# An fp32 transformer step on one Trainium2 core: token tiles finished one by one, side work and copies reordered, router products turned, slot rows on another queue

## The reference

```python
def first_block(x, ...):
    h = layer_norm(x, ln_in_g, ln_in_b)
    for l in range(2):
        m = hybrid_mixer(h, w_in[l], cmp_pos[l], cmp_w1[l], ..., w_o[l])
        h = layer_norm(ALPHA * h + m, ln1_g[l], ln1_b[l])
        if l % 2 == 0:
            f = swiglu(h, ffn_wg[0], ffn_wu[0], ffn_wd[0])              # 1024 -> 2816 -> 1024
        else:
            f = moe_swiglu(h, moe_router[0], moe_wg[0], moe_wu[0], moe_wd[0])
        h = layer_norm(ALPHA * h + f, ln2_g[l], ln2_b[l])
    return h

def hybrid_mixer(h, w_in, ...):
    q, kc, vc, ks, vs, kw, vw, gates, u, bg, cg = jnp.split(h @ w_in, offsets, axis=-1)
    # q goes to three attentions: over compressed keys (an MLP over blocks of kc, vc),
    # over selected blocks (ks, vs), over a window (kw, vw); u, bg, cg to a short convolution
    return jnp.concatenate([o_attn, o_conv], axis=-1) @ w_o

def moe_swiglu(h, w_router, wg, wu, wd):
    top_v, top_i = lax.top_k(h @ w_router, 2)                           # 8 logits a token
    gate = jnp.sum(jax.nn.one_hot(top_i, 8) * softmax(top_v)[..., None], axis=-2)
    return sum(gate[..., e:e + 1] * swiglu(h, wg[e], wu[e], wd[e]) for e in range(8))

def second_block(x, c, ...):
    shift, scale, gate = jnp.split(silu(c) @ w_mod + b_mod, 3, axis=-1)
    h = rms_norm(x, g_norm) * (1.0 + scale) + shift
    # projections of h; convolution and RG-LRU; rotary dilated attention in three groups
    x = x + gate * (merged @ w_o)
    return rms_norm(x, g_final)
```

## Time and profile before

| | |
|---|---|
| runs | 2350.46, 2355.13, 2360.42 us (median 2355.13) |
| the profiled execution | 2353.95 us; its span 2352.1 us |
| granted TensorE clock, mean | 0.988 |
| busy: PE | 2294.8 us, 98% |
| busy: PEld (weight loads) | 1824.2 us, 78% |
| busy: DVE (VectorE) | 1459.4 us, 62% |
| busy: ACT (ScalarE) | 1185.2 us, 50% |
| busy: POOL (GpSimd) | 553.8 us, 24% |
| DMA | 435.51 MB, mean 185 GB/s |

### The profile page before, as it was taken

One profiled execution on the slowest core, in us unless ns is written; L12 is line 12 of the kernel. 1 busy time (PEld: TensorE's weight loads), 2 busy tenths in 40 slices (PEclk: granted clock), 3 DMA queues, 4 the chain that ended last, 5 costly groups with the idle time before them and its releaser, 6 DMA issues.

```text
span 2352.1 us, 30586 instructions
## 1 busy us (share of the span) xinstructions
PE 2294.8 (98%) x11059; PEld 1824.2 (78%) x11059; DVE 1459.4 (62%) x2159; ACT 1185.2 (50%) x1625; POOL 553.8 (24%) x230
## 2 busy tenths in 40 slices
PE   7999999999999999999999999999989999999998
PEld 5766777788888766688888888888866788788787
DVE  5277674621163576688889888898887572245333
ACT  4344342222233444377778777777764652334323
POOL 4212334544422221210000000000023344433342
PEclk9999999999999999999999999999998999999999
DMA  8211237823324211379999999999982233322232
GB/s 231 54 46 46 72 108 244 277 78 97 106 85 126 61 45 43 138 281 375 369 388 381 384 366 379 387 386 379 356 315 63 72 99 100 95 65 72 71 91 72
DMA packets 321096, 435.51 MB, mean 185 GB/s; under 512 B 15024, under 2 KB 259168, under 8 KB 320992
## 3 DMA queue, kind: packets, MB, share of 16 engines
q1 hardware_dynamic: 301356, 402.58, 49.1%
q10 hardware_dynamic: 17332, 23.17, 3.2%
q0 software_dynamic: 2304, 8.39, 0.9%
HBM read 409.97 MB, written 22.02 MB: 184 GB/s over the span
## 4 chain that ended last, share of the span: by engine, by line
PE 86%; DVE 6%; DMA 4%; ACT 2%; issue 1%; ACTq 0%; DVEq 0%; SPq 0%
PE bank L841 21%; PE bank L1284 18%; PE bank L845 10%; PE bank L1295 8%; PE bank L1463 6%; PE bank L1158 5%; DMA mod_raw<-in_w_mod_dram 2%; PE bank L1194 2%; PE bank L1133 2%; PE bank L1175 2%; DMA raw_m<-in_moe_wu_dram 1%; PE bank L1303 1%; DVE mod_sum L2255 1%; PE bank L1042 1%; PE bank L882 1%
## 5 line engine op out<-in xcount | busy, mean ns | idle before, releaser
L778 POOL TENSOR_TENSOR rest<-raw,head 128x1024 fp32r<-128x1024 f32 (+1 forms) x210 | 529.8, 2528 | 1025.3 <-ACT head L1593 997.2
L2543 DVE TENSOR_TENSOR rest_m<-raw_m,head_m 128x1408 fp32r<-128x1408 f32 (+1 forms) x405 | 576.4, 1458 | 86.0 <-ACT head_m L1663 81.3
L1663 ACT ACTIVATE head_m<-raw_m 128x1408 fp32r<-128x1408 f32 (+1 forms) x405 | 495.6, 1251 | 111.1 <-DMA raw_m<-in_moe_wu_dram 38.6
L1593 ACT ACTIVATE head<-raw 128x1024 fp32r<-128x1024 f32 (+1 forms) x210 | 225.7, 1077 | 247.8 <-PE bank L845 178.0
L841 PE MATMUL bank<-HH,head 128*128 128x512 f32 x760 | 307.0, 404 | 8.3 <-ACT head L1593 4.2
L841 PE MATMUL bank<-HL,head 128*128 128x512 f32 x760 | 301.2, 396 | 0.0
L1284 PE MATMUL bank<-head_m,XH 128*128 128x512 f32 x720 | 277.0, 385 | 0.7 <-DVE rest_m L2543 0.7
L1284 PE MATMUL bank<-head_m,XL 128*128 128x512 f32 x720 | 270.4, 375 | 0.0
L1284 PE MATMUL bank<-rest_m,XH 128*128 128x512 f32 x720 | 270.3, 375 | 0.0
L845 PE MATMUL bank<-HH,rest 128*128 128x512 f32 x760 | 192.7, 395 | 0.0
L841 PEld LDWEIGHTS bank<-HH,head 128*128 128x128 f32 x760 | 143.0, 188 | 49.0 <-issue 10.8
(11 more groups left out here) (459 smaller groups left out, 3845.6 us busy)
## 6 DMA issues: line engine op xcount, KB each, us to landing
raw_m<-in_moe_wg_dram SPq DMA_DIRECT2D x120, 704.0 KB, 8.0
raw_m<-in_moe_wu_dram SPq DMA_DIRECT2D x120, 704.0 KB, 7.0
raw_m<-in_moe_wd_dram SPq DMA_DIRECT2D x165, 512.0 KB, 5.2
raw<-in_w_in_dram SPq DMA_DIRECT2D x110, 512.0 KB, 4.0
raw<-in_w_o_dram SPq DMA_DIRECT2D x24, 512.0 KB, 4.0
mod_raw<-in_w_mod_dram ACTq DMA_DIRECT2D x12, 1024.0 KB, 6.6
raw<-in_ffn_wg_dram SPq DMA_DIRECT2D x22, 512.0 KB, 3.9
raw<-in_ffn_wu_dram SPq DMA_DIRECT2D x22, 512.0 KB, 3.9
```

The source lines that it names most:

```text
L778: pool.tensor_tensor(rest[slot][:, 0:kt, :], raw[slot][:, 0:kt, :], head[slot][:, 0:kt, :], ALU.subtract).then_inc(weights_split, 1)
L1593: act.activation(head[slot][:, 0:kt, :], raw[slot][:, 0:kt, :], ACT.Copy).then_inc(head_done, 1)
L1663: act.activation(head_m[at_ % HEADS_M][:, 0:w], raw_m[at_ % RAWS][:, 0:w], ACT.Copy) \
L2543: dve.tensor_tensor(rest_m[at_ % RAWS][:, 0:w], raw_m[at_ % RAWS][:, 0:w], head_m[at_ % HEADS_M][:, 0:w], ALU.subtract).then_inc(gran_spli ...
```

## The change

1. **Token tiles one by one.** For each of the four tiles statistics and offset (VectorE), root and normalization (ScalarE) are written together; VectorE now normalizes the whole of the last tile.
2. **Vector loads.** The seven on ScalarE's queue go to SP's, behind `vectors_in`'s own, and SP waits for token tile 1 ahead of the first weight tile.
3. **Query bank.** Query tile 0 is taken ahead of the copies from K in both layers.
4. **Side work.** `side_loads(j - 1)` stands ahead of the copy of `UH[j]`, and `mod_chunk(j - 1)` is summed after pair j.
5. **Norms.** Two subtractions are written ahead of the wait for the deviation.
6. **Router.** The tokens are the stationary side, the 8 weight columns the moving one: 32 products of 8 columns, whose result already has tokens on the partitions; `lgT`, its copy and the four transposes are gone, and the semaphore counts with them.
7. **Slot rows.** Those of slot 1 are issued by ScalarE, ahead of its last silu of slot 0; SP goes on with its granules.

```diff
+RAW_BEHIND = 1
-STAT_AT = [1, 2, 4, 7]
-OFF_AT = [3, 5, 6, 8]
+STAT_AT = [1, 3, 5, 7]
+OFF_AT = [2, 4, 6, 8]
...
                 for g in range(first):
                     granule(g, owner[0])
-                sp.wait_ge(x_scattered, 16 * 2 * ST)
-                slot_rows(1)
                 stored = 0
...
-                for name, rows in VECTORS[VECTORS_SP:]:
+                for name, rows in VECTORS[EARLY:]:
+                    if name == "b2dup":
+                        continue
...
+                if l == 0:
+                    sp.wait_ge(sem_x[RAW_BEHIND], 16)
                 for k, c in enumerate(order):
...
                 for k in range(KT):
                     pe.wait_ge(h_ready, 2 * KT + k + 1)
-                    last = pe.matmul(bank[6][0:EXPERTS, :], rw[:, k, :], H[:, k, :], start=(k == 0), stop=(k == KT - 1))
+                    for t in range(ST):
+                        last = pe.matmul(bank[6][:, t * EXPERTS:(t + 1) * EXPERTS], H[:, k, t * P:(t + 1) * P], rw[:, k, :],
+                                         start=(k == 0 and t == 0), stop=(k == KT - 1 and t == ST - 1))
...
-                for q in range(2):
+                for q in range(2 * ST):
                     tokens(q)
+
                 pe.wait_ge(lg_ready, 2)
-                for t in range(ST):
-                    last = pe.transpose(bank[7][:, t * EXPERTS:(t + 1) * EXPERTS], lgT[:, t * P:(t + 1) * P],
-                                        cst[0:EXPERTS, 0:EXPERTS])
-                last.then_inc(lg_done, 1)
-                for q in range(2, 2 * ST):
-                    tokens(q)
-
-                pe.wait_ge(lg_ready, 3)
                 ranks = bank[7][:, 64:64 + TE]
...
-            for name, rows in VECTORS[EARLY:VECTORS_SP]:
-                if name != "b2dup":
-                    st, row = WHERE[name] // P, WHERE[name] % P
-                    act.dma_start(stage[row:row + rows, st, :], vector_sources(a, name)).then_inc(sem_stage, 16)
...
+                act.wait_ge(x_scattered, 16 * 2 * ST)
+                act.dma_start(xs[1][:, :], x_rows[P:2 * P, :]).then_inc(xs_landed[1], 16)
                 silu(0, KT - 1)
-                act.wait_ge(x_scattered, 16 * 2 * ST)
...
-            x_root(0)
-            x_root(1)
-            x_normed(0, 0, D)
-            x_root(2)
-            x_normed(1, 0, D)
-            x_normed(2, 0, S)
-            x_root(3)
-            x_normed(2, S, D)
-            x_normed(3, S, D)
+            for t in range(ST - 1):
+                x_root(t)
+                x_normed(t, 0, D)
+            x_root(ST - 1)
...
                         ahead(e, 2 * j + 1)
+                        if after and j >= 1:
+                            after(j - 1)
                         act.wait_ge(bank_free[(n + 1) % RING], e * (N_PART // RING) + (n + 1) // RING + 1)
                         act.activation(UH[:, j, :], gu[:, j % 2, :], ACT.Copy).then_inc(uh_ready, 1)
-                        if after:
-                            after(j)
+                    if after:
+                        after(PT - 1)
...
-            x_statistics(0)
-            x_statistics(1)
-            x_offset(0)
-            dve.wait_ge(par_T, 1)
-            dve.tensor_copy(par[:, 0:EARLY_ROWS], bank[7][:, 0:EARLY_ROWS]).then_inc(par_ready, 1)
-            x_statistics(2)
-            x_offset(1)
-            x_offset(2)
-            x_statistics(3)
-            x_offset(3)
+            for t in range(ST):
+                x_statistics(t)
+                x_offset(t)
+                if t == 0:
+                    dve.wait_ge(par_T, 1)
+                    dve.tensor_copy(par[:, 0:EARLY_ROWS], bank[7][:, 0:EARLY_ROWS]).then_inc(par_ready, 1)
             dve.wait_ge(x_stats, OFF_AT[3])
-            dve.tensor_scalar(x_tok[:, 3, 0:S], x_tok[:, 3, 0:S], xsd[:, 3:4], xof[:, 3:4], ALU.mult, ALU.add) \
+            dve.tensor_scalar(x_tok[:, 3, :], x_tok[:, 3, :], xsd[:, 3:4], xof[:, 3:4], ALU.mult, ALU.add) \
...
                 products(dve, L, N_SPREAD)
+                for k in range(2):
+                    step(dve.tensor_tensor(H[:, k, :], H[:, k, :], bank[4][:, :], ALU.subtract))
+                products(dve, L, N_RSTD)
                 for k in range(KT + 1):
                     if k < KT:
-                        step(dve.tensor_tensor(H[:, k, :], H[:, k, :], bank[4][:, :], ALU.subtract))
-                        if k == 0:
-                            products(dve, L, N_RSTD)
+                        if k >= 2:
+                            step(dve.tensor_tensor(H[:, k, :], H[:, k, :], bank[4][:, :], ALU.subtract))
...
-                if l == 1:
-                    query_taken(0)
+                query_taken(0)
                 dve.wait_ge(dup_c, 64 * (l + 1))
...
-                dve.tensor_copy(lgT[:, :], bank[6][0:EXPERTS, :]).then_inc(lg_ready, 1)
-                dve.wait_ge(lg_done, 3)
-                step(dve.tensor_copy(lg[:, :, :], bank[7][:, 0:TE].rearrange("p (t e) -> p t e", e=EXPERTS)))
+                step(dve.tensor_copy(lg[:, :, :], bank[6][:, 0:TE].rearrange("p (t e) -> p t e", e=EXPERTS)))
...
-                    if j < PT - 2:
-                        mod_chunk(j)
+                    if 1 <= j < PT - 1:
+                        mod_chunk(j - 1)
```

28 lines of the change are left out of this document (11 added, 17 removed).

## The result

The changed kernel takes 2358.08 us (median of 15 runs, 2355.72 to 2361.74), the kernel before 2352.5 (15 runs, 2350.46 to 2360.42): a ratio of 1.0018, 95% interval 1.0011 to 1.0025. By the ratio it is slower by 4.2 us (the medians lie 5.6 apart), where 7 us faster were forecast, and it lies 2 us above the range's upper end. The profiled execution took 2359.88 us, its span 2358.1, 6.0 more than before.

A forecast was written before the change was run, and what follows sets the result against it. TensorE was taken as the bound, 86% of the span, so edits pay only at its gaps or half clock. Terms -5.0 + 1.4 + 0.6 - 0.7 - 4.0 - 1.0 + 1.7 = -7.0 took 2353.95 to 2347.0 us; range 2340 to 2356.

The forecast's parts named there:

- The gated part's step: First gated part: load issued before the product is waited for, sum a step behind, waiting falls beside TensorE's tile; -4.0 us.
- The token tiles: Start: statistics, root and normalization tile by tile; 0 us, ends -1 and +1, covered by TensorE's later wait.
- the norms: Two subtractions ahead: norm 1 +0.6 us, norm 2 0, norm 3 -0.7.
- The query step: Query bank, block 1: TensorE's 3.2 us wait for the query copy and 1.8 of half clock go; -5.0 us.
- The loads: Start: seven vector loads on SP's queue make the fourth weight tile, and so the fifth, later; +1.4 us, between 0 and 2.5.
- worst case: Start: TensorE's wait is 1.5 us instead of 0.4 and brings half clock; +1.8 us.
- The router: Router: logits copy and four transposes gone, so what arrives at the rank product is -1.0 us, between 0 and -1.4.
- so they are covered: Router: a column's four products, 1.05 us, hide behind VectorE's step of 1.32.
- Rival 2: Router runs at half clock, last step and 32 transposes cost more: +4.7 us, 2351.7; chance 0.14.
- The slot rows: Slots: granules flowing beside the scatter slow it, TensorE gets granule 13 later; +1.7 us, ends +0.4 and +3.5.
- Rival 4: Slots: the scatter starves beside full granule queue, TensorE loses 10.7 us: 2356; decides from a loss of 8.7; chance 0.08.
- the 5 that the prediction counted as cover: Gated part: VectorE's slack in a pair, 11.2 - 6.0 = 5 us, as cover if the moved loads were late.

The follow-up runs named there:

- four kept: The changed kernel with edits 2, 6 and 7 undone, so edits 1, 3, 4 and 5 kept: 2344.92 us, ratio 0.9949 to the kernel before.
- two granules: The kernel before with edits 3 and 4 alone, SP issuing 14 granules in place of 12 ahead of its wait for the scatter: 2348.02 us, ratio 0.9976.
- SP waits: The changed kernel, ScalarE still issuing slot 1's rows, but SP also waiting for the scatter before granule 13: 2351.74 us, ratio 0.9985 to the kernel before.
- no tile wait: The changed kernel without SP's wait for token tile 1 ahead of the first weight tile, vector loads still on SP: 2355.95 us, ratio 1.001.
- the run with both products: The changed kernel with the old router product computed beside the new ones, into a bank nobody reads: 2374.61 us, ratio 1.0057 to the kernel before.

## Why the prediction was wrong

**What was right.** The gains: edits 3 and 4 were to bring -5.0 and -4.0, and without the others they bring -9.0 by the medians. Neither was run by itself. The gated part's step holds as it was put; its size, -4.8 to -5.2 for -4.0, lies at the far bound of -5.0. The token tiles (0) hold too, and the norms (-0.1 forecast in sum, under 0.5 by undoing). The query step's size was luck, though: 3.2 us of wait and the low clock stood in the one trace that I had, and in the second the wait was 0.3. By 80 us the four traces with edit 3 and without edit 2 are 3.3 to 4.5 ahead of the first trace before, but only 0.1 to 1.3 ahead of the second.

**What was wrong** are three small terms, +1.4, -1.0 and +1.7, in sum +2.1. Undone together they are worth 13.2 (2358.1 to 2344.9), one by one 3.6, 5.8 and 5.5, in sum 14.9; by the ratios it is 16 and 17. That covers the error to be explained, 11.1 (2358.1 for 2347.0).

*The loads* ("+1.4, between 0 and 2.5"). The delay of the fourth tile's issue was right to 0.1 us (1.46). That it would arrive at the fifth tile no larger was wrong: the landing moved by 3.4. The step that failed is the 2.2 us that I took off because SP idled there. SP idled, but its queue was moving the constants, and these went out 3.6 later. Then TensorE stopped for 3.0 us and the clock fell, the "worst case" of +1.8 that I named and left out. In the runs edit 2 costs 3.6 to 4.1.

*The router* ("-1.0, between 0 and -1.4"). The step that failed is "so they are covered". It compared 1.05 for four products with VectorE's 1.32, a price at 2.4 GHz, although had the clock at 0.52 up to 993.8, over the first half of the router. At 1.2 GHz four products cost 1.72, more than 1.32, and TensorE became the bound for eight columns. Rival 2 had the place and the clock, and priced only the last step and the transposes: 4.7; undoing the edit gave 5.8 in the medians and 4.1 in the trace. Other traces give less: from 972 to 1012 us the six with the old router lie 2.6 earlier to 0.0 later than the first trace before, on average 0.8 earlier, the seven with the new one 0.1 earlier to 3.7 later, on average 1.6 later. That is 2.4 for the place itself, forecast -1.0; another 2.3 of the 5.8 lie at the slot rows, where the kernel with edit 6 undone lost less, and the last 1.1 is not located. The Trainium skill's rule on weight loads (TensorE: Matmul & The Clock Gate, "LDWEIGHTS"), that their time goes by the columns, had pointed there: PEld is busy 13.76 of 13.80 us in the changed router at 1.2 GHz, 5.64 of 13.50 in the old one at 2.4.

What my sum left out altogether, and only rival 2 had, is that the clock is low for longer with the new router. At 1.2 GHz from norm 3's last sums to the end of the router, in us:

| router | executions traced | time at 1.2 GHz |
|---|---|---|
| old, 8 x 512 columns | before (twice); edits 3, 4; four kept; two granules; edit 6 undone | 10.2, 3.4, 10.3, 10.2, 10.2, 6.9 |
| new, 32 x 8 columns | the change; edits 7, 2, 5, 4 undone; SP waits; no tile wait | 23.9, 17.1, 17.0, 20.4, 23.9, 20.5, 20.5 |

In five of these seven the clock had risen to 2.4 GHz and fell again among the columns' products; with the old router it never did there. Here it is in the kernel with edit 7 undone, at 2.4 GHz and then for 13.7 us at 1.2:

```profile
985.10:988.50 3.40, 2.04 (x18) 1.96 (x17) 3.33 (x6) 2.33 (x3) 0.00 (x0) 1.00 1.02 422
988.50:1002.20 13.70, 13.70 (x65) 13.70 (x66) 8.88 (x24) 5.86 (x8) 0.00 (x0) 0.50 0.50 204
```

That the 8-column products go with a low clock, all seven show. Part of it comes back: at the start of the first slot's picking (1007.2 to 1010.6 in the first trace before) five of the six with the old router have 3.4 us more at 1.2 GHz, of the seven with the new one only one. What in these products makes the clock fall is open, since the run with both products fits neither simple answer.

*The slot rows* ("+1.7, between +0.4 and +3.5"). The mechanism was the forecast's own, the granules beside the scatter, and both of its parts were too small. The scatter ended 2.2 later (24.1 against 21.9 from its first issue), where 1.3 were forecast. The rate was right: beside the full granule queue the scatter moved 1.60 MB in 9 us, 0.18 a us, as in the earlier trace rows. The amount was too small: I let that rate hold for the last 0.82 MB alone, while in the kernel with edit 7 undone, whose first granules go out as early as the changed one's, 1.15 MB were left when the granules ran thin (from 1025.6 us), and its scatter took 3.0 less. And the rows, which I had landing at 1039, were used at 1043.8: they took 7.8 us from issue to landing in place of 3.7, with granules moving beside them. Then the long stop cost 10.3 us at 1.2 GHz. Rival 4 had that mechanism, and 10.7 for its price; 5.5 to 6.9 was measured, so it fell short of its own point of decision, 8.7. The Trainium skill (DMA: Bandwidth & Descriptors, "SWDGE vs HWDGE vs iDMA") says that a DMA engine serves software and hardware queues in turn; the 43.5% of q0 above agrees.

**The chances.** Each rival was priced as if the rest went as forecast. Two of them, 0.14 and 0.08, came about together, the second at two thirds of its price, and with a worst case; no case of mine held that. In all three places TensorE stops or runs small products and a stretch at 1.2 GHz is there, so I should not have taken them as independent; no run shows how they hang together. The range ended at 2356, where rivals 2 and 4 with the worst case of the loads, 4.7 + 9.0 + 1.8 on 2347.0 (rival 4's 2356 is 9.0 above it), would have given 2362.5.

**Norm 1**, +3.2 in the ledger, can't be put down to the change: all thirteen other traces have 6.8 to 13.7 us at 1.2 GHz there, the kernel before itself 6.8 in its second, and their losses at the place go from 0.4 to 3.2, with edit 5 or without. The first trace was the exception.

## What to carry over

Price an edit on TensorE at the clock that the trace shows over that very stretch, and ask whether the longer step still hides behind its neighbour; a saving on VectorE is worth nothing if the products behind it become the bound. A queue that stands still beside a slow transfer may be making way for it: before it is freed, count what will flow in its place and what will then stand ahead of the next urgent load. An engine's idle time is not its queue's: before it is taken as slack, see what transfers run in it. And take a gap from more than one execution before counting its removal, and bundle no sure gain with doubtful ones: two of the seven edits, alone, were worth 9 us, all seven together cost 4 to 6.

## What the runs showed of the hardware

- VectorE's side work slows beside GpSimd's subtractions. Seven steps of the weighted sum took 3.61 us before, when GpSimd rested; with the change they overlap with its work. From the changed kernel:

```profile
374.47 7.87 DVE L2237 SCALAR_TENSOR_TENSOR mod_sum<-mod_raw,c_act,mod_sum 128x256 f32<-128x256 f32 x7
374.47 2.40 POOL L779 TENSOR_TENSOR rest<-raw,head 128x1024 fp32r<-128x1024 f32 x1 [4.65 <-ACT head L1581]
```

Two of the seven took 2.68 and 2.55 us in place of 0.48; each had begun beside one of GpSimd's subtractions (2.40) and ended 0.3 after it. The four copies from K took 1.79 us in eight of the fourteen traces, where they were done or nearly done when GpSimd's next subtraction began, and 3.97 to 10.02 in the six others. The eight are those with edit 2, in which the fifth weight tile, and with it GpSimd's work on it, comes later. Within the kernel before it was 7.01 and 3.97: that makes the query gap a matter of luck. The Trainium skill (SBUF — State Buffer, "SBUF: two separate sides") has a rule for it: an fp32 copy within SBUF, or an operation with two SBUF inputs, takes a port pair that GpSimd also needs, and the one that comes later stands still for the whole of the other's instruction; the 2.68 beside 2.40 agrees. VectorE's slack in a pair of the gated part is thus 11.2 - 8.2 - 1.4 = 1.6 us, not the 5 that the prediction counted as cover.

- The granted clock's stretches differ between executions of one kernel: norm 1 of the kernel before had 3.4 us at 1.2 GHz in one and 6.8 in the other, norm 3 had 10.2 and 3.4, while the two times, 2353.95 and 2352.6, are close. A difference of a few us at one such place needs more than one trace on either side.
